# A recurrent layer's sigmoids written as tanh of half the argument, with a clamp on GpSimd ahead of the square root

## The reference, cut to what matters

```python
def rg_lru(u, gate_w, gate_b, lam):          # u: [1, 256, 1536], 12 heads of 128
    g = jnp.einsum('bshi,hio->bsho', uh, gate_w) + gate_b
    g = jax.nn.sigmoid(g.astype(jnp.float32))
    r = g[..., :LRU_BLOCK].reshape(bsz, s, w)
    i = g[..., LRU_BLOCK:].reshape(bsz, s, w)
    log_a = -LRU_C * r * jax.nn.softplus(-lam.astype(jnp.float32))   # LRU_C = 8
    a = jnp.exp(log_a)
    mult = jnp.sqrt(-jnp.expm1(2.0 * log_a))
    bterm = mult * (i * u.astype(jnp.float32))
    _, h = lax.associative_scan(combine, (a, bterm), axis=1)   # h_t = a_t h_(t-1) + bterm_t

def recurrent_mixer(h, w_in, conv_w, conv_b, gate_w, gate_b, lam, w_out):
    u = jnp.einsum('bsd,dc->bsc', h, w_in)
    gate, xb = u[..., :WIDTH], u[..., WIDTH:]
    xb = causal_depthwise_conv(xb, conv_w, conv_b)
    y = rg_lru(xb, gate_w, gate_b, lam)
    return jnp.einsum('bsc,cd->bsd', y * jax.nn.silu(gate), w_out)
```

## Time and profile before

| | before |
|---|---|
| median of 3 runs | 872.07 us (871.88 to 872.14) |
| the profiled execution's own time | 873.84 us |
| its span, first to last instruction | 871.7 us |
| PE busy | 856.8 us, 98% |
| DVE busy | 677.4 us, 78% |
| ACT busy | 549.5 us, 63% |
| POOL busy | 26.9 us, 3% |
| the recurrent layer in the trace | about 583 to 691 us from the span's start |

### The profile page before, as it was taken

One profiled execution on the slowest core, in us unless ns is written; L12 is line 12 of the kernel. 1 busy time (PEld: TensorE's weight loads), 2 busy tenths in 40 slices (PEclk: granted clock), 3 DMA queues, 4 the chain that ended last, 5 costly groups with the idle time before them and its releaser, 6 DMA issues.

```text
span 871.7 us, 13362 instructions
## 1 busy us (share of the span) xinstructions
PE 856.8 (98%) x4881; PEld 750.2 (86%) x4881; DVE 677.4 (78%) x969; ACT 549.5 (63%) x752; POOL 26.9 (3%) x48
## 2 busy tenths in 40 slices
PE   8999999999999999999899999999999999999997
PEld 8978789888888888889788888989899798888886
DVE  6898767887877798867788877787887777776764
ACT  5855556656656575575665665568998865555543
POOL 2000100000000041010000000000000000000000
PEclk9999999999999999999999999999999999999999
DMA  8553533665555344226656556535265046545511
GB/s 321 199 194 139 194 145 121 221 220 211 192 200 186 145 164 174 97 97 217 241 194 209 182 190 207 176 115 223 102 236 195 0 147 242 214 174 213 207 58 48
DMA packets 22731, 152.79 MB, mean 175 GB/s; under 512 B 2560, under 2 KB 2688, under 8 KB 5408
## 3 DMA queue, kind: packets, MB, share of 16 engines
q1 hardware_dynamic: 22320, 149.71, 47.7%
q0 software_dynamic: 368, 2.49, 0.8%
HBM read 151.14 MB, written 1.05 MB: 175 GB/s over the span
## 4 chain that ended last, share of the span: by engine, by line
PE 79%; DVE 8%; ACT 3%; DMA 2%; issue 1%; DVEq 0%; ACTq 0%; SPq 0%
PE acc L1824 27%; PE ring L1758 22%; PE ring L1762 12%; PE ring L1811 7%; DVE w_lo L990 3%; PE acc L2043 3%; DMA raw<-in_stream_dram 2%; PE ring L2025 1%; DVE hh L1057 1%; ACT w_hi L501 1%; PE ring L2083 1%; PE ring L2201 1%; PE acc L1725 1%; PE ring L1773 1%; DVE cacc L1303 1%
## 5 line engine op out<-in xcount | busy, mean ns | idle before, releaser
L990 DVE TENSOR_TENSOR w_lo<-raw,w_hi 128x2048 fp32r<-128x2048 f32 (+1 forms) x145 | 318.1, 2198 | 5.6 <-ACT w_hi L501 5.5
L501 ACT ACTIVATE w_hi<-raw 128x2048 fp32r<-128x2048 f32 (+1 forms) x146 | 266.9, 1840 | 54.7 <-DMA raw<-in_stream_dram 51.4
L1758 PE MATMUL ring<-hh,w_hi 128*128 128x512 f32 x944 | 235.8, 392 | 0.7 <-DVE usum L1108 0.7
L1758 PEld LDWEIGHTS ring<-hh,w_hi 128*128 128x128 f32 x944 | 171.3, 189 | 32.6 <-issue 0.9
L1762 PEld LDWEIGHTS ring<-hh,w_lo 128*128 128x128 f32 x944 | 128.8, 190 | 9.2
L1762 PE MATMUL ring<-hh,w_lo 128*128 128x256 f32 x944 | 131.6, 282 | 0.0
L1824 PE MATMUL acc<-w_hi,a_hi 128*128 128x512 f32 x264 | 104.4, 395 | 2.4 <-DVE a_lo L1333 2.4
L1824 PE MATMUL acc<-w_lo,a_hi 128*128 128x512 f32 x264 | 103.8, 393 | 0.0
L1824 PE MATMUL acc<-w_hi,a_lo 128*128 128x512 f32 x264 | 103.4, 392 | 0.0
L1108 DVE TENSOR_TENSOR usum<-ring,usum 128x512 f32<-128x512 f32 x65 | 44.8, 689 | 63.2 <-ACT usum L506 63.0
L1811 PE MATMUL ring<-hh,w_hi 128*128 128x256 f32 x480 | 87.7, 285 | 0.8 <-DVE gg L1572 0.8
(11 more groups left out here) (247 smaller groups left out, 961.6 us busy)
## 6 DMA issues: line engine op xcount, KB each, us to landing
raw<-in_stream_dram SPq DMA_DIRECT2D x134, 1024.0 KB, 4.8
raw<-in_stream_dram SPq DMA_DIRECT2D x12, 512.0 KB, 3.9
gatew<-in_gatew_dram POOLq DMA_DIRECT2D x1, 1536.0 KB, 7.0
x<-in_x_dram SPq DMA_DIRECT2D x2, 512.0 KB, 3.8
out_dram<-xn SPq DMA_DIRECT2D x4, 256.0 KB, 2.2
row<-in_row_dram POOLq DMA_DIRECT2D x1, 640.0 KB, 9.8
gup_raw<-in_gup_dram SPq DMA_DIRECT2D x3, 128.0 KB, 13.8
par<-in_par_dram SPq DMA_DIRECT2D x1, 274.0 KB, 4.7
```

The costliest lines, as they stand in the source:

```text
L501: nc.scalar.activation(w_hi[:, u % RING, 0:n], raw[:, u % RAW, 0:n], ACT.Copy).then_inc(hi_split, 1)
L990: nc.vector.tensor_tensor(w_lo[:, u % RING, 0:n], raw[:, u % RAW, 0:n], w_hi[:, u % RING, 0:n].bitcast(f32), ALU.subtract).then_inc(lo_spl ...
L1758: nc.tensor.matmul(ring[:, 2 * k + f, :], w_hi[:, u % RING, lo:lo + P], hh[:, kc, :, :], start=kc == 0, stop=False, skip_group_check=True)
```

## The change

All three sigmoids of the recurrent layer become `Tanh` of half the argument (the identity is sigmoid(z) = (1 + tanh(z / 2)) / 2). The gates take half the bias from a new tile `half_bias`; the tanh and the exponential of the decay take their factor as scale and as bias; `1 + tanh` is made inside the DVE products, and the factor 4 that results is taken out by the root's scale of 1/16. Since rounding could bring the root's argument below zero, GpSimd clamps `ug` at zero, in place, and the root waits for that (`clamped`).

```diff
@@ gpsimd
             rms_of_x("lru")
+            for e in range(LRU_ITERS):
+                pool.wait_ge(tanh_ready, 2 * e + 2)
+                nc.gpsimd.tensor_scalar(ug[:, :, :], ug[:, :, :], 0.0, None, ALU.max).then_inc(clamped, 1)
             rms_of_x("sc")
@@ scalar, gates (last_gates alike)
+                if e == 0:
+                    act.wait_ge(sp_ready, 1)
...
-                        c = C_LGB + 2 * (2 * e + k) + r
+                        c = 2 * (2 * e + k) + r
                         last = nc.scalar.activation(buf[:, k, :], ring[:, HEAD_BANKS[k], r * S:(r + 1) * S],
-                                                    ACT.Sigmoid, bias=par[:, c:c + 1])
+                                                    ACT.Tanh, scale=0.5, bias=half_bias[:, c:c + 1])
@@ scalar, tanhs
-                if e == 0:
-                    act.wait_ge(sp4_ready, 1)
...
-                    nc.scalar.activation(ug[:, k, :], rg[:, k, :], ACT.Tanh, scale=sp4[:, h:h + 1]).then_inc(tanh_ready, 1)
+                    nc.scalar.activation(ug[:, k, :], rg[:, k, :], ACT.Tanh, scale=sp2[:, h:h + 1],
+                                         bias=sp2[:, h:h + 1]).then_inc(tanh_ready, 1)
@@ scalar, decays
-                    nc.scalar.activation(aa[:, k, :], rg[:, k, :], ACT.Exp, scale=sp8[:, h:h + 1]).then_inc(decay_ready, 1)
+                    nc.scalar.activation(aa[:, k, :], rg[:, k, :], ACT.Exp, scale=sp4[:, h:h + 1], bias=sp4[:, h:h + 1]).then_inc(decay_ready, 1)
@@ scalar, roots
-                act.wait_ge(tanh_ready, 2 * e + 2)
+                act.wait_ge(clamped, e + 1)
                 for k in parts:
-                    nc.scalar.activation(su[:, k, :], ug[:, k, :], ACT.Sqrt).then_inc(sqrt_ready, 1)
+                    nc.scalar.activation(su[:, k, :], ug[:, k, :], ACT.Sqrt, scale=1.0 / 16).then_inc(sqrt_ready, 1)
@@ scalar, gated
-                nc.scalar.activation(sgate[:, :, :], gate, ACT.Sigmoid).then_inc(gate_ready, 1)
+                nc.scalar.activation(sgate[:, :, :], gate, ACT.Tanh, scale=0.5).then_inc(gate_ready, 1)
@@ vector, setup
-            own.mark(nc.vector.tensor_scalar(sp8[:, :], lam_p[:, :], -LRU_C, None, ALU.mult))
-            nc.vector.tensor_scalar(sp4[:, :], lam_p[:, :], LRU_C / 2, None, ALU.mult).then_inc(sp4_ready, 1)
+            own.mark(nc.vector.tensor_scalar(half_bias[:, :], par[:, C_LGB:C_LGB + 2 * LRU_HEADS], 0.5, None, ALU.mult))
+            own.mark(nc.vector.tensor_scalar(sp4[:, :], lam_p[:, :], -LRU_C / 2, None, ALU.mult))
+            own.wait()
+            nc.vector.tensor_scalar(sp2[:, :], lam_p[:, :], LRU_C / 4, None, ALU.mult).then_inc(sp_ready, 1)
@@ vector, inputs_gated and lru_gate
-                nc.vector.tensor_tensor(iu[:, :, :], ig[:, :, :], xc[:, :, :], ALU.mult).then_inc(branch_used, 1)
+                nc.vector.scalar_tensor_tensor(out=iu[:, :, :], in0=ig[:, :, :], scalar=1.0, in1=xc[:, :, :],
+                                               op0=ALU.add, op1=ALU.mult).then_inc(branch_used, 1)
...
-                nc.vector.tensor_tensor(gg[:, :, :], gate, sgate[:, :, :], ALU.mult).then_inc(gate_free, 1)
+                nc.vector.scalar_tensor_tensor(out=gg[:, :, :], in0=sgate[:, :, :], scalar=1.0, in1=gate,
+                                               op0=ALU.add, op1=ALU.mult).then_inc(gate_free, 1)
```

More of the change, by code:

```diff
@@ L218, in two_block_kernel @@
         stat, mean, rstd = (put(n, [P, 20]) for n in ("stat", "mean", "rstd"))
-        sp4, sp8, lam_e, lam_s, lam_q, lam_p = (put(n, [P, LRU_HEADS]) for n in ("sp4", "sp8", "lam_e", "lam_s", "lam_q", "lam_p"))
+        sp2, sp4, lam_e, lam_s, lam_q, lam_p = (put(n, [P, LRU_HEADS]) for n in ("sp2", "sp4", "lam_e", "lam_s", "lam_q", "lam_p"))
+        half_bias = put("half_bias", [P, 2 * LRU_HEADS])
         xn_at = top
@@ L319, in two_block_kernel @@
         o_ready, o_free = sem("o_ready"), sem("o_free")
-        lam_ready, sp4_ready = sem("lam_ready"), sem("sp4_ready")
+        lam_ready, sp_ready, clamped = sem("lam_ready"), sem("sp_ready"), sem("clamped")
         ri_ready, tanh_ready, decay_ready, sqrt_ready = (sem(n) for n in ("ri_ready", "tanh_ready", "decay_ready", "sqrt_ready"))
```

## The result

| | before | changed |
|---|---|---|
| median of 15 runs each, same chip | 872.14 us | 874.85 us |
| spread | 871.12 to 872.94 | 873.76 to 879.24 |
| ratio, 95% interval | | 1.0038 (1.0028 to 1.0047) |
| the profiled execution's own time | 873.84 us | 874.39 us |
| its span | 871.7 us | 872.3 us |

What follows compares the result with a forecast made beforehand. TensorE was taken to bound the kernel. A gain of 0.89 us at its stop in the recurrent layer and 0.20 us lost in setup gave -0.69 us: 871.38 against a median of 872.07, range 870.9 to 872.9.

Steps and rivals of the forecast that it cites:

- The bound: Whole kernel: TensorE is busy for 856.8 of 871.7 us, so time can be won only where it stands still.
- the layer's one stop: TensorE's wait behind the eight gate matmuls of step 2 in the recurrent layer, 1.15 us, the most to win back.
- The sum, -0.89 + 0.20: Whole kernel: 0.89 us gained at TensorE's stop, 0.20 us lost in setup, together -0.69 us, giving 871.38 us.
- Table loads: ACT, recurrent layer: six fewer loads, 1.28 us each, 7.7 us of ACT's time, worth nothing except in step 1.
- Step 1 without a clamp: Recurrent layer: the product with the root starts at 609.50 instead of 610.39, a gain of 0.89 us, leaving 0.26 stop.
- The clamp's length: GpSimd's clamp of ug: 0.66 us taken from one-input rows, with 1.48 us from above by a two-input row.
- Who goes first: Step 1, clamp at 604.24 against DVE's iu due at 604.31: iu was taken to go first, the clamp costing nothing.
- the rival's 0.26 to 0.66: Clamp goes first in step 1, chance 0.30: iu slips by 0.26 to 0.66 us, total about 871.85 us.
- Setup: Before the first mixer: one more DVE instruction and a wait lose 0.20 us, which nothing later gives back.
- ACT's busy time: Sign to look for on ACT: six loads fewer, busy time down by about 6 us.
- The slower rival: Step 1, chance 0.10: a 1.48 us clamp goes first, iu slips by 1.48, 0.79 us lost, 872.86 us.

## Why the prediction was wrong, point by point

- **The bound.** TensorE bounds the kernel, and the layer's one stop was the right place to look. But "time can be won only where it stands still" was read as if time could be lost only there too. TensorE lost its time while it ran.
- **The sum, -0.89 + 0.20.** This is the step that failed. It has a term for every instruction that the diff adds and none for the tile that it adds. The 128 bytes of `half_bias` cost 3.3 us alone (872.07 to 875.37), by longer matmuls in stages that the change does not touch. Without them the same change measured 0.8 us faster than the kernel before (0.1 to 2.2 by its interval). That this lies near the sum's 0.69 is luck: with the clamp in first place the term -0.89 was -0.48, and the two terms give 0.27. None of my rivals named the move, so the range missed as well.
- **Table loads.** Right: six fewer, worth 0 except in step 1. No drain shows behind a load, as forecast: the root started at 608.48, 1.29 us behind its load at 607.19.
- **Step 1 without a clamp.** Right: a remaining stop of 0.26 us was forecast, 0.24 measured in both kernels without clamps.
- **The clamp's length.** 1.49 to 2.04 us, where I took 0.66 from the one-input rows and kept 1.48 as the upper end from a two-input row. The upper end was the value. As forecast, no root waited for it.
- **Who goes first.** I gave `iu` the better chance and was wrong: a lead of 0.05 us was enough for the clamp. `iu` slipped by 0.42, inside the rival's 0.26 to 0.66, and the stop of 0.67 is that rival's. In step 2 both began at 618.14, `iu` took its normal 0.69 and the clamp 2.04.
- **Setup.** Right: 0.20 forecast, TensorE's wait 0.21 longer.
- **ACT's busy time.** 6.9 us less; I had said about 6.
- **The slower rival** (a slow clamp in first place, 872.86) put its loss at the wrong mechanism. The clamp was as slow as it supposed, but it held `iu` for 0.42 us and not for its whole length, so it cost 0.4 us, which is less than the gain.

## What to carry to other kernels

A new tile in a layout made by adding up sizes moves everything behind it, and here the 128 bytes of a small bias tile cost more than all the instructions of the change. Before costing a change, compare the addresses of the operands that the bounding engine reads; put small new tiles at the end, or into free columns, or pad so that the large operands stay a multiple of 256 bytes apart. The runs here show this for float32 matmuls of 512 columns and the distances in the table, no others. When a matmul-bound kernel loses time with no new wait, compare the time of a fixed run of matmuls in stages that the change does not touch.

## What the runs showed of the hardware that I had not expected

- Matmuls whose weight operand stood 128, 320 or 384 bytes (modulo 512) from the moving operand ran at 232 to 234 ns from start to start, those at distance 0 or 256 at 228: about 2% in 816 float32 matmuls of 512 columns, 3 to 4 us per execution. Those with `hh` as weights stood at distance 0 throughout and kept a median of 226 to 227 in all fourteen traces.
- The stretch from 404 to 440 us, where weight units land late, took TensorE 32.3 to 35.9 us in fourteen traces of fourteen kernels, a spread as large as the whole loss and without order by kernel. The profiled execution before had the longest.
- A GpSimd `tensor_scalar` with one constant operand on 128x512 float32 took 1.49 us, 2.9 ns per element, three times the 0.96 ns per further element of the affine_select rows.
- A 0.69 us DVE instruction with two SBUF inputs that began 0.05 us behind that clamp lost 0.42 us and ended at 605.06, while the clamp ran on to 605.40. The Trainium skill (SBUF — State Buffer, "Who interferes with whom") has the one that issues first keep the ports for its whole length; in step 1 the order agrees with this trace, the length does not, as far as the profiler's rough spans on GpSimd tell. In step 2, where both began at 618.14, `iu` took its normal 0.69 and the clamp 2.04.
